# Fifth projection as full-precision products inside attention's first steps, and query norms as multipliers of the scores

## The chip, the cores and the metric

One core of a Trainium2 chip runs the whole program. The time is the device time of one execution in microseconds. TensorE (PE) does matrix products and transposes, VectorE (DVE) and ScalarE (ACT) do elementwise work, GpSimd (POOL) is hardly used, and SyncE (SP) issues the loads.

## The reference, cut to what matters

Two layers, each FFN, hybrid mixer, FFN, over 256 tokens of width 1024. The mixer projects the normed input `u` by `w_in` and splits it:

```python
    (a_q, a_k, a_v, b_cq, b_ckv, b_kr, c_q,
     c_kc, c_vc, c_ks, c_vs, c_kw, c_vw, c_gf) = jnp.split(u @ w_in, splits, axis=-1)
    qa = apply_rope(rms_norm(heads(a_q, A_HEADS), a_qk_g[0]), cos64, sin64)
    ka = apply_rope(rms_norm(heads(a_k, A_KV_HEADS), a_qk_g[1]), cos64, sin64)
...
    qc = rms_norm(heads(c_q, C_HEADS), c_qk_g[0])
    qc_rot = apply_rope(qc, cos64, sin64)
    k_cmp = rms_norm(compress_blocks(...), c_qk_g[1])
    k_slc = apply_rope(rms_norm(heads(c_ks, C_KV_HEADS), c_qk_g[2]), cos64, sin64)
    k_win = apply_rope(rms_norm(heads(c_kw, C_KV_HEADS), c_qk_g[3]), cos64, sin64)
```

Branch a is banded attention with sinks, branch b latent attention, branch c attends to compressed keys (`qc` with `k_cmp`), to selected blocks and to a window (`qc_rot` with `k_slc`, `k_win`). Scores are divided by the root of the head's width before the softmax; a norm of a query is one number per token and head, so it can be applied to the query or to its scores.

## The kernel before, in words

All in fp32. Each engine has one queue, written out by hand, and waits on semaphores; TensorE's products run in the order of its queue. Tokens are two tiles of 128.

The mixer has five projections (`CHUNKS`: F_LAT, F_CMPIN, F_A, F_CQ, F_CK). The first three (`project`, L845) use the fp32 operands as they are; a product of 128x128 by 128x512 is then two instructions. F_CQ (the queries of branch c) and F_CK (its keys and values, 512 columns) use `project_split`: ScalarE rounds the weights into `mwh` quarter by quarter (`round_rows`, L1327), VectorE makes the remainders `mwl` (`rest_rows`, L1915), and TensorE makes three products per block of rounded parts (L861, L862, L866). Both go to PSUM banks 2 and 3. `copy_proj` squares and copies the results for the norms (F_CK: L1277, L1279, into `ck2` and `pk`).

Small products and transposes use banks 4 to 7 as a ring: the names in `AUX` are numbered, number g uses bank 4 + g % 4, and `aux_open` waits until the result of number g - 4 has been taken out by the engine named beside it. The semaphores count in the order of the list. Before the change it has cq0, cq1 (numbers 23, 24), cmps0, cmps1, cr0, cr1, ks, kw, cmpt: transposed cq, compressed scores, transposed roped queries (from `qr`), transposed keys, transposed compressed probabilities.

Attention runs over twelve units n of two heads (two of a, two of b, eight of c). A unit goes through `scores` (TensorE, L890), `rescore` (VectorE, L1980 and L1982: scale, mask and row minimum in one custom operation), `exponents` (ScalarE, L1370 and L1371), `normalise` (VectorE, L1991 to L1997), `turn_probs` (transposes, L901), `turned_probs` (ScalarE's copy, L1378), `values` (L924, L926) and, with its neighbours, `mix_out`, the output projection (L723, L725, L727), whose first piece stands in step n = 4 and waits for `cmpt`. Further work is woven in: in step 1 the compressed scores (L1063) on TensorE and, on VectorE after `rescore(1)`, `key_norms`, then `normalise(1)` and `key_ropes`; in step 2 the transposes of `qr` (L878) and of the keys, and `compressed_scores` (L2020 to L2024) on VectorE after `rescore(2)`; in step 3 `compressed_probs`.

Query and key norms are made by `heads_rstd` (sum of squares, then eight small steps in `rsqrt`) and multiplied in by `by_rstd` (L1510; for cq L1945).

Of the kernel before, what the change touches and what calls it, by code (L numbers as in the profile page):

```python
# [33 lines left out]
I32 = mybir.dt.int32  # L34
# [40 lines left out]
CHUNKS = (F_LAT, F_CMPIN, F_A, F_CQ, F_CK)  # L75
# [6 lines left out]
       ("cq0", "act"), ("cq1", "act"), ("cmps0", "dve"), ("cmps1", "dve"), ("cr0", "act"), ("cr1", "act"),  # L82
# [28 lines left out]
def hybrid_kernel(nc, x, c, positions, ada_w, ada_b, norm_g, ffn_w_in, ffn_w_out, w_in, w_out,  # L111
                  a_sinks, a_qk_g, b_q_lat_g, b_kv_lat_g, b_w_uq, b_w_ukv, b_qk_nope_g, b_qk_rope_g,
                  c_qk_g, c_cmp_pe, c_cmp_w1, c_cmp_w2, c_gate_w, c_gate_b, consts, out):
    with ExitStack() as ctx:
# [122 lines left out]
        def ET(n, i):  # L237
# [6 lines left out]
        csc = fa[:, :, 0:C_H * NCMP].rearrange("p a (h b) -> p a h b", h=C_H)  # L244
        trg = cqT[:, 0:3, :].rearrange("p a n -> p (a n)")
        kwt = sb("kwt", [P, SEQ])
        cst16 = sb("cst16", [P, 3, NT * C_H])
# [35 lines left out]
        muh_ready, mul_ready_, mwh_ready, mwl_ready, mwh_used = (  # L283
            sem(n) for n in ("muh_ready", "mul_ready_", "mwh_ready", "mwl_ready", "mwh_used"))
# [46 lines left out]
        def quarter_at(l, fill, q):  # L331

            return 8 * l + (0 if fill == F_CQ else 4) + q + 1
# [9 lines left out]
        PREP = ["lat", "qb", "kb", "qa", "kc", "cq", "cr", "ck", "cmp"]  # L343
# [38 lines left out]
        def head(n, i):  # L382
# [3 lines left out]
            if br == "a":  # L386
                return (qaT[half, hh // 2, :], kaT[half, hh // 2, :],
                        lambda t: pa[:, t, 384 + hh // 2 * HD:384 + hh // 2 * HD + HD], cst[:, C_BAND:C_CAUSAL + P], SC64)
            if br == "b":
                return qbT[:, hh, :], kbT[:, hh, :], lambda t: kvb[:, t, hh, HD:P], mlate[:, :], SC96  # L390
# [4 lines left out]
                    lambda t: pk[:, t, off:off + HD], mlate[:, :], SC64)  # L395
# [13 lines left out]
        def _(sp):  # L409
# [21 lines left out]
            def ffn_wide(l, f, b, c):  # L431
# [4 lines left out]
                elif f == 1:  # L436
                    sp.wait_ge(proj, projected(l, (F_CQ, F_CK)[b]))
# [169 lines left out]
        def _(pe):  # L607
# [225 lines left out]
            def project(l, fill, width, banks):  # L833
# [4 lines left out]
                if c >= 2:  # L838

                    pe.wait_ge(pcopy, l * 2 * len(CHUNKS) + 2 * (c if fill == F_CK else c - 1))  # L840
# [10 lines left out]
            def project_split(l, fill, banks):  # L851

                n, c = WIDE_M + fill, CHUNKS.index(fill)
                pe.wait_ge(pcopy, l * 2 * len(CHUNKS) + 2 * (c if fill == F_CK else c - 1))
                pe.wait_ge(muh_ready, l + 1)
                pe.wait_ge(mul_ready_, l + 1)
                for q in range(4):
# [12 lines left out]
                    if q < 3 and fill == F_CQ:  # L870
                        i.then_inc(mwh_used, 1)
# [73 lines left out]
            def mixer(l):  # L945
# [3 lines left out]
                pe.wait_ge(pcopy, l * 10 + 4)  # L949
# [74 lines left out]
                turn(l, "kc", [(P * g, kcd[:, g, :, :].rearrange("p a n -> p (a n)")) for g in range(2)])  # L1024
                pe.wait_ge(*aux_done("ka", l))
                pe.wait_ge(pcopy, l * 10 + 6)
                scores(l, 0)
                project_split(l, F_CK, 2)
                cq = pq[:, :, :].rearrange("p t (a n) -> p t a n", a=C_H)

# [1080 lines left out]
```

## Time and profile before

| | |
|---|---|
| median of 3 runs | 1129.51 us (1128.81 to 1130.82) |
| the profiled execution | 1130.08 us, of which 1128.3 is the span |
| TensorE busy | 1084.1 us (96%) |
| VectorE busy | 831.3 us (74%) |
| ScalarE busy | 499.5 us (44%) |
| granted TensorE clock | 0.989 |

Times in the rows are in us from the start of the span, durations in us unless marked ns. A matmul's record is longer than the distance to the next, since they overlap: the rate is read from starts. "PEclk" is the granted share of TensorE's full clock. Idle time in brackets is the engine's own before the instruction, with what ended it.

### The profile page before, as it was taken

What the parts mean: (1) busy time and instruction counts of PE and PEld (TensorE: products, weight loads), DVE (VectorE), ACT (ScalarE), POOL (GpSimd) and SP (SyncE); (2) the same over time, 40 slices, a digit from 0 to 9 for tenths busy, and PEclk for the clock granted to TensorE, in tenths of its full rate; (3) what the DMA queues carried; (4) which work ended last, traced back from release to release, by engine and by line L of the source; (5) the groups of instructions that cost most, each with busy time, mean ns of one, the idle gap of its engine ahead of it and who ended that gap; (6) DMA issues with size and microseconds to landing.
All of it is one profiled execution on the core that took longest, in us unless ns stands there. A gap on an engine that the chain in (4) does not pass through costs nothing.

```text
span 1128.3 us, 13797 instructions
## 1 busy us (share of the span) xinstructions
PE 1084.1 (96%) x5221; PEld 837.4 (74%) x5221; DVE 831.3 (74%) x1502; ACT 499.5 (44%) x868; POOL 12.0 (1%) x30
## 2 busy tenths in 40 slices
PE   5999999999989999999999999999998999999998
PEld 1688888865766588888878888886576667888887
DVE  1766997886988785876687789886879787655644
ACT  2543342324567563343534433422255566433431
POOL 4000000000000000000000000000000000000000
PEclk9999999999989999999999999999998999999999
DMA  9799999454612179896439999954582113876631
GB/s 360 259 378 363 372 378 326 148 180 129 224 62 76 38 252 330 305 325 209 162 113 334 342 387 384 355 194 156 115 294 80 53 61 115 269 250 230 199 112 74
DMA packets 149366, 253.70 MB, mean 225 GB/s; under 512 B 9639, under 2 KB 119861, under 8 KB 141109
## 3 DMA queue, kind: packets, MB, share of 16 engines
q1 hardware_dynamic: 148596, 251.53, 65.1%
q10 hardware_dynamic: 704, 1.30, 0.3%
q8 instruction: 41, 0.67, 0.2%
q14 instruction: 25, 0.20, 0.1%
HBM read 251.76 MB, written 1.05 MB: 224 GB/s over the span
## 4 chain that ended last, share of the span: by engine, by line
PE 84%; DVE 11%; ACT 2%; issue 1%; DMA 1%; SPq 0%; DVEq 0%; ACTq 0%
PE ps L693 12%; PE ps L695 12%; PE ps L694 12%; PE ps L723 8%; PE ps L727 8%; PE ps L725 8%; PE ps L845 6%; DVE mwl L1915 2%; PE ps L705 2%; PE ps L674 1%; PE ps L672 1%; PE ps L673 1%; PE ps L901 1%; DMA wide<-in_ada_w_dram 1%; PE ps L890 1%
## 5 line engine op out<-in xcount | busy, mean ns | idle before, releaser
L693 PE MATMUL ps<-wh,uh 128*128 128x512 f32 x576 | 227.2, 395 | 0.0
L695 PE MATMUL ps<-wlo,uh 128*128 128x512 f32 x576 | 224.5, 390 | 0.0
L694 PE MATMUL ps<-wh,ul 128*128 128x512 f32 x576 | 224.3, 389 | 0.0
L1645 DVE TENSOR_TENSOR wlo<-wide,wh 128x1024 fp32r<-128x1024 f32 x176 | 207.6, 1220 | 15.7 <-ACT wh L1183 13.9
L1183 ACT CAST wh<-wide 128x1024 fp32r<-128x1024 f32 x176 | 175.9, 1049 | 16.7 <-DMA wide<-in_ffn_w_in_dram 16.7
L1255 ACT ACTIVATE fs<-ps 128x512 f32<-128x512 f32 x40 | 24.0, 599 | 282.3 <-PE ps L695 273.1
L1800 DVE TENSOR_TENSOR fa<-fs,ps 128x512 f32<-128x512 f32 x40 | 27.5, 688 | 137.8 <-ACT fs L1255 137.2
L723 PE MATMUL ps<-th,fh 128*128 128x512 f32 x320 | 128.1, 400 | 0.0
L695 PEld LDWEIGHTS ps<-wlo,uh 128*128 128x128 f32 x576 | 108.1, 188 | 23.0
L727 PE MATMUL ps<-tlo,fh 128*128 128x512 f32 x320 | 125.0, 390 | 0.0
L725 PE MATMUL ps<-th,fl 128*128 128x512 f32 x320 | 124.6, 390 | 0.0
L694 PEld LDWEIGHTS ps<-wh,ul 128*128 128x128 f32 x576 | 108.3, 188 | 21.6
L693 PEld LDWEIGHTS ps<-wh,uh 128*128 128x128 f32 x576 | 108.2, 188 | 21.4
L1673 DVE TENSOR_TENSOR tlo<-tall,th 128x1024 fp32r<-128x1024 f32 x104 | 123.4, 1219 | 0.0
L1656 DVE SCALAR_TENSOR_TENSOR acc<-ada,cond,acc 128x2048 f32<-128x2048 f32 (+1 forms) x49 | 100.2, 2044 | 22.9 <-DMA ada<-in_ada_w_dram 22.5
L1190 ACT CAST th<-tall 128x1024 fp32r<-128x1024 f32 x104 | 105.2, 1051 | 10.8 <-DMA tall<-in_ffn_w_out_dram 10.8
L725 PEld LDWEIGHTS ps<-th,fl 128*128 128x128 f32 x320 | 60.2, 188 | 12.7 <-issue 1.0
L727 PEld LDWEIGHTS ps<-tlo,fh 128*128 128x128 f32 x320 | 60.0, 188 | 12.8
L723 PEld LDWEIGHTS ps<-th,fh 128*128 128x128 f32 x320 | 60.1, 188 | 12.6 <-issue 1.0
L845 PE MATMUL ps<-wide,u 128*128 128x416 f32 (+2 forms) x192 | 68.6, 515 | 0.3
L845 PEld LDWEIGHTS ps<-wide,u 128*128 128x128 f32 x192 | 36.0, 190 | 29.5 <-issue 23.6
L1195 ACT CAST fh<-ps 128x512 fp32r<-128x512 f32 x40 | 23.5, 587 | 60.3 <-PE ps L705 60.3
(363 smaller groups left out, 1548.2 us busy)
## 6 DMA issues: line engine op xcount, KB each, us to landing
wide<-in_ffn_w_in_dram SPq DMA_DIRECT2D x176, 512.0 KB, 6.6
ada<-in_ada_w_dram SPq DMA_DIRECT2D x60, 1024.0 KB, 7.1
tall<-in_ffn_w_out_dram SPq DMA_DIRECT2D x44, 1024.0 KB, 5.2
wide<-in_w_in_dram SPq DMA_DIRECT2D x14, 1024.0 KB, 7.5
tall<-in_w_out_dram SPq DMA_DIRECT2D x8, 1024.0 KB, 8.6
ada<-in_ada_w_dram SPq DMA_DIRECT2D x16, 512.0 KB, 5.9
wide<-in_c_cmp_w_dram SPq DMA_DIRECT2D x4, 1024.0 KB, 10.1
wide<-in_w_in_dram SPq DMA_DIRECT2D x4, 832.0 KB, 7.9
```

Source lines behind the costliest of these rows:

```text
L693: mm(o, uh[:, k, rows_], wh[:, hsl, :, k, :], start=(k == 0), stop=False, skip_group_check=True)
L694: mm(o, ul[:, k, rows_], wh[:, hsl, :, k, :], start=False, stop=False, skip_group_check=True)
L695: i = mm(o, uh[:, k, rows_], wlo[:, s, :, k, :], start=False, stop=(k == KD - 1), skip_group_check=True)
L723: mm(y[:, t, hf, :], hi[:, toks], th[:, slot, a, cols], start=(first and x == 0), stop=False, skip_group_check=True)
L725: mm(y[:, t, hf, :], lo[:, toks], th[:, slot, a, cols], start=False, stop=False, skip_group_check=True)
L727: i = mm(y[:, t, hf, :], hi[:, toks], tlo[:, slot, a, cols], start=False, stop=(last and x == len(rows) - 1), skip_group_check=True)
L845: i = mm(ps[:, banks + t, 0:width], u[:, k, t * P:(t + 1) * P], wv[:, k, :], start=(k == 0), stop=(k == KD - 1))
L1183: nc.scalar.copy(wh[:, (n + 1) % 2, :, 2 * c:2 * c + 2, :], raw).then_inc(wh_ready, 1)
L1190: nc.scalar.copy(th[:, n % 2, m % 2, :], tall[:, n % 2, m % 2 * DM:(m % 2 + 1) * DM]).then_inc(th_ready, 1)
L1645: tt(wlo[:, n % 2, :, ks, :], raw, wh[:, (n + 1) % 2, :, ks, :].bitcast(F32), ALU.subtract)\
L1656: stt(part, piece, cond[:, k:k + 1], part, ALU.mult, ALU.add).then_inc(ada_used, 1)
L1673: tt(tlo[:, n % 2, m % 2, :], tall[:, n % 2, m % 2 * DM:(m % 2 + 1) * DM], th[:, n % 2, m % 2, :].bitcast(F32), ALU.subtract).then_inc(tl_ ...
```

## The change

F_CK leaves `CHUNKS`. Its roundings, remainders and split products are gone, and `key_rows` makes it of plain fp32 products in the ring's banks, one tile per name: ck0 after `scores(0)`, ck1 in step 1 after the compressed scores. `copy_keys` takes them out on ScalarE. `AUX` becomes cq0, cq1, ck0, cmps0, cmps1, ck1, cr0, cr1, ks, kw, cmpt (numbers 23 to 33). The cq transposes move ahead of `scores(0)`.

The queries of a and c stay unnormed. `score_root` makes minus the reciprocal root of the sum of squares (the scale of the scores included) into `aroot` and `qroot`, and `rescore` takes it as a per-token multiplier. For the compressed scores it is multiplied in as a tensor, and maximum becomes minimum. Keys of a are still normed, with a table factor of -8.

```diff
-CHUNKS = (F_LAT, F_CMPIN, F_A, F_CQ, F_CK)
+CHUNKS = (F_LAT, F_CMPIN, F_A, F_CQ)
...
-       ("cq0", "act"), ("cq1", "act"), ("cmps0", "dve"), ("cmps1", "dve"), ("cr0", "act"), ("cr1", "act"),
+       ("cq0", "act"), ("cq1", "act"), ("ck0", "act"), ("cmps0", "dve"), ("cmps1", "dve"), ("ck1", "act"), ("cr0", "act"), ("cr1", "act"),
...
-        csc = fa[:, :, 0:C_H * NCMP].rearrange("p a (h b) -> p a h b", h=C_H)
+        csc = ada[:, 0, 0:NT * C_H * NCMP].rearrange("p (a h b) -> p a h b", a=NT, h=C_H)
...
-                    sp.wait_ge(proj, projected(l, (F_CQ, F_CK)[b]))
+                    sp.wait_ge(*((proj, projected(l, F_CQ)), (aux_ready, aux_at(l, "ck1")))[b])
...
+            def key_rows(l, t):
+
+                name = f"ck{t}"
+                bank = aux_open(l, name)
+                n = WIDE_M + F_CK
+                wv = wide[:, n % 2, :].rearrange("p (k n) -> p k n", k=KD)
+                if t == 0:
+                    wide_wait(pe, l, n)
+                for k in range(KD):
+                    i = mm(bank, u[:, k, token(t)], wv[:, k, :], start=(k == 0), stop=(k == KD - 1))
+                i.then_inc(aux_ready, 1)
...
+                pe.wait_ge(pcopy, l * 8 + 8)
+                cq = pq[:, :, :].rearrange("p t (a n) -> p t a n", a=C_H)
+                pairs("cq0", cq, (0, 1))
+                pairs("cq1", cq, (2, 3))
                 pe.wait_ge(*aux_done("ka", l))
                 scores(l, 0)
-                project_split(l, F_CK, 2)
+                key_rows(l, 0)
                 for n in range(1, NU + 3):
...
-                    if n == 1:
-                        pe.wait_ge(prep, prep_at(l, "cq"))
-                        pairs("cq0", cq, (0, 1))
-                        pairs("cq1", cq, (2, 3))
-                        pe.wait_ge(pcopy, l * 10 + 10)
...
+                        key_rows(l, 1)
                     if n == 2:
                         pe.wait_ge(prep, prep_at(l, "ck"))
...
+            def copy_keys(l, t):
+
+                aux_wait(l, f"ck{t}")
+                src = ps[:, aux_bank(f"ck{t}"), :].rearrange("p (a b n) -> p a b n", a=2, b=2)
+                A(ck2[:, t, :].rearrange("p (a n) -> p a n", a=2), src[:, :, 0, :], ACT.Square)
+                nc.scalar.copy(pk[:, t, :].rearrange("p (b a n) -> p a b n", a=2, b=2), src).then_inc(aux_act, 1)
...
-                for q in range(3):
-                    round_rows(F_CK, q)
...
-                round_rows(F_CK, 3)
-
+                out_of(l, "cq0", cqT[:, 0:2, :])
+                out_of(l, "cq1", cqT[:, 2:4, :])
...
-                copy_proj(l, 4)
+                copy_keys(l, 0)
...
+                        if n == 1 and i == 1:
+                            copy_keys(l, 1)
...
+            def score_root(root, sums):
+
+                p, a, n, d = sums.shape
+                link(V.tensor_reduce(ssb[:, 0:a * n].rearrange("p (a n) -> p a n", a=a), sums, AX.X, ALU.add))
+                link(ts(ssb[:, 0:a * n], ssb[:, 0:a * n], HD * EPS, None, ALU.add))
+                rsqrt(a * n, root=root[:, :])
+                return root[:, :].rearrange("p (a n) -> p a n", a=a)
...
-                tt(c[:, 0, :, :], cs64[:, 0, :, :], g(0, HD), ALU.mult)
+                stt(c[:, 0, :, :], cs64[:, 0, :, :], by, g(0, HD), ALU.mult, ALU.mult)
...
-                heads_rstd(qk, HD, v4(qk2[:, :, :], 6))
-                by_rstd(qk, qk)
+                root = score_root(aroot, v4(qk2[:, :, :], 6))[:, :, A_H:6].unsqueeze(3).broadcast_to([P, NT, A_KV, HD])
+                link(tt(qk[:, :, A_H:6, :], qk[:, :, A_H:6, :], root, ALU.mult))
...
-                for q in range(3):
-                    rest_rows(F_CK, q)
                 copied(l, 3)
                 cq = v4(pq, C_H)
-                heads_rstd(cq, HD, v4(cq2[:, :, :], C_H))
...
-                tt(cq, cq, r, ALU.mult).then_inc(prep, 1)
-                dve.wait_ge(prep, prep_at(l, "cq"))
-                rest_rows(F_CK, 3)
+                roots = score_root(qroot, v4(cq2[:, :, :], C_H))
...
-                    V.tensor_tensor_reduce(e[:, 0:P], ps[:, i, 0:P], cst[:, C_CAUSAL:C_CAUSAL + P], -scale, least,
+                    V.tensor_tensor_reduce(e[:, 0:P], ps[:, i, 0:P], cst[:, C_CAUSAL:C_CAUSAL + P], scale[0], least,
...
                 def key_norms():
-                    copied(l, 4)
+                    dve.wait_ge(*aux_done("ck1", l))
...
-                    link(V.tensor_reduce(over(0), csc, AX.X, ALU.max))
+                    link(tt(csc, csc, roots.unsqueeze(3).broadcast_to([P, NT, C_H, NCMP]), ALU.mult))
+                    link(V.tensor_reduce(over(0), csc, AX.X, ALU.min))
```

## Rows read from the trace of the kernel before

**Rows 1.** The page, busy time, share of the span, instructions.

```profile
PE 1084.1 (96%) x5221; PEld 837.4 (74%) x5221; DVE 831.3 (74%) x1502; ACT 499.5 (44%) x868; POOL 12.0 (1%) x30
```

**Rows 2.** The chain of waits by time, 225 to 335: start, us, what.

```profile
260.00 13.93 PE ps L845 x32
...
292.93 3.50 DVE mwl L1915 x3
296.43 1.14 DVE ssb L1503
...
299.48 1.24 DVE acc L1945
300.74 1.23 DVE mwl L1915
...
305.81 0.35 DVE acc L1980
...
308.88 0.17 DVE stat L1991
...
331.68 0.48 ACT cmpT L1295
```

**Rows 3.** Timeline of TensorE: start, us, engine, line, count, [idle before].

```profile
295.41 0.93 PE L890 MATMUL ps<-kaT,qaT 64*128 64x128 f32 x8 [1.57 <-ACT kaT L1295]
...
311.40 2.65 PE L1063 MATMUL ps<-kcT,cqT 64*128 64x15 f32 x32 [0.47 <-ACT cqT L1295]
...
314.68 2.77 PE L890 MATMUL ps<-kbT,qbT 96*128 96x128 f32 x8
317.24 1.91 PE L878 MATMUL ps<-cst,qr 128*128 128x128 f32 x8
...
319.97 0.55 PE L901 MATMUL ps<-cst,early 128*128 128x128 f32 x3
...
332.25 0.47 PE L723 MATMUL ps<-th,uh 128*128 128x512 f32 x1 [2.20 <-ACT cmpT L1295]
```

**Rows 4.** Windows: length, then busy time of each engine, granted clock, DMA share.

```profile
312.00:320.00 8.00, 8.00 (x53) 6.84 (x51) 7.47 (x32) 3.45 (x12) 0.00 (x0) 0.57 0.43 138
320.00:332.00 12.00, 7.87 (x61) 5.49 (x59) 11.46 (x50) 9.56 (x30) 0.00 (x0) 1.00 0.01 1
332.00:337.00 5.00, 4.75 (x15) 3.71 (x15) 2.72 (x10) 1.41 (x6) 0.00 (x0) 0.66 0.00 0
337.00:382.00 45.00, 43.64 (x277) 29.77 (x276) 35.93 (x134) 30.14 (x83) 0.00 (x0) 1.00 0.21 71
```

**Rows 5.** Timeline of VectorE.

```profile
249.34 0.88 DVE L1858 TENSOR_SCALAR latT<-ps,latg 128x256 f32<-128x256 f32 x2 [0.16 <-PE ps L878]
...
281.49 2.36 DVE L1915 TENSOR_TENSOR mwl<-wide,mwh 128x1024 fp32r<-128x1024 f32 x2 [2.72 <-ACT mwh L1327]
...
311.09 0.68 DVE L1503 TENSOR_REDUCE ssb<-ck 128x8 f32<-128x512 f32 x1
...
320.11 0.47 DVE L2020 TENSOR_TENSOR fa<-ps,cst 128x120 f32<-128x120 f32 x2
...
322.16 0.15 DVE L1992 RECIPROCAL stat<-stat 128x2 f32<-128x2 f32 x1
```

**Rows 6.** Timeline of ScalarE.

```profile
293.78 0.60 ACT L1287 COPY acc<-ps 128x512 f32<-128x512 f32 x1
...
309.75 0.57 ACT L1279 COPY acc<-ps 128x512 f32<-128x512 f32 x1
...
320.56 0.48 ACT L1378 COPY acc<-ps 128x384 f32<-128x384 f32 x1 [0.78 <-PE ps L901]
...
321.82 0.39 ACT L1370 ACTIVATE acc<-acc,stat 128x128 f32<-128x128 f32 x1
```

**Rows 7.** Groups by form, 286 to 332: count, busy, mean ns of one.

```profile
L1980 DVE CUSTOM_DVE_ANT_0 acc<-ps,cst,nsink 128x128 f32<-128x128 f32 x2 | 0.7, 350 | 0.0
...
L1980 DVE CUSTOM_DVE_ANT_0 acc<-ps,cst 128x128 f32<-128x128 f32 x2 | 0.6, 290 | 0.0
```

More of the change, by code:

```diff
@@ L282, in hybrid_kernel @@
         chain_s = sem("chain")
-        muh_ready, mul_ready_, mwh_ready, mwl_ready, mwh_used = (
-            sem(n) for n in ("muh_ready", "mul_ready_", "mwh_ready", "mwl_ready", "mwh_used"))
+        muh_ready, mul_ready_, mwh_ready, mwl_ready = (
+            sem(n) for n in ("muh_ready", "mul_ready_", "mwh_ready", "mwl_ready"))
         gu_t0, ft_t0, fh_t0, fl_t0 = (sem(n) for n in ("gu_t0", "ft_t0", "fh_t0", "fl_t0"))
@@ L331, in quarter_at @@
         def quarter_at(l, fill, q):
-            return 8 * l + (0 if fill == F_CQ else 4) + q + 1
+            return 4 * l + q + 1
         def row_at(l, j, t):
@@ L387, in head @@
                 return (qaT[half, hh // 2, :], kaT[half, hh // 2, :],
-                        lambda t: pa[:, t, 384 + hh // 2 * HD:384 + hh // 2 * HD + HD], cst[:, C_BAND:C_CAUSAL + P], SC64)
+                        lambda t: pa[:, t, 384 + hh // 2 * HD:384 + hh // 2 * HD + HD], cst[:, C_BAND:C_CAUSAL + P],
+                        [aroot[:, 6 * t + hh:6 * t + hh + 1] for t in range(NT)])
             if br == "b":
-                return qbT[:, hh, :], kbT[:, hh, :], lambda t: kvb[:, t, hh, HD:P], mlate[:, :], SC96
+                return qbT[:, hh, :], kbT[:, hh, :], lambda t: kvb[:, t, hh, HD:P], mlate[:, :], [-SC96, -SC96]
             win = int(br == "win")
@@ L394, in head @@
             return (crT[half, hh // 2, :], ckT[half, 2 * win + kv, :],
-                    lambda t: pk[:, t, off:off + HD], mlate[:, :], SC64)
+                    lambda t: pk[:, t, off:off + HD], mlate[:, :],
+                    [qroot[:, C_H * t + hh:C_H * t + hh + 1] for t in range(NT)])
         def head_at(l, n, i):
@@ L1324, in round_rows @@
                     act.wait_ge(wide_in[n % 2][q // 2], wide_at(l, n))
-                    if fill == F_CK and q < 3:
-                        act.wait_ge(mwh_used, 3 * l + q + 1)
                     nc.scalar.copy(mwh[:, ks, :], wide[:, n % 2, :].rearrange("p (k n) -> p k n", k=KD)[:, ks, :])\
@@ L1400, in mixer @@
                             act.wait_ge(cmp_shift, l + 1)
-                            A(csc, csc, ACT.Exp, scale=SC64).then_inc(cmp_exp, 1)
+                            A(csc, csc, ACT.Exp, scale=-1.0).then_inc(cmp_exp, 1)
                         if n == 4 and i == 0:
@@ L1483, in link, with rsqrt @@
                 dve.wait_ge(chain_s, chain["n"])
-            def rsqrt(n, p=P):
-                s, t, r = ssb[0:p, 0:n], newt[0:p, 0:n], rst[0:p, 0:n]
-                link(ts(r.bitcast(I32), s.bitcast(I32), -0.5, float(0x5F3759DF), ALU.mult, ALU.add))
+            def rsqrt(n, p=P, root=None):
+                s, t, r = ssb[0:p, 0:n], newt[0:p, 0:n], rst[0:p, 0:n] if root is None else root
+                seed = float(0x5F3759DF) if root is None else float(0x5F3759DF - 2 ** 31)
+                link(ts(r.bitcast(I32), s.bitcast(I32), -0.5, seed, ALU.mult, ALU.add))
                 link(tt(t, r, r, ALU.mult))
@@ L1979, in rescore @@
                         dve.wait_ge(pt_ready, head_at(l, n - 2, i))
-                    V.tensor_tensor_reduce(e[:, 0:P], ps[:, i, 0:P], cst[:, C_CAUSAL:C_CAUSAL + P], -scale, least,
+                    V.tensor_tensor_reduce(e[:, 0:P], ps[:, i, 0:P], cst[:, C_CAUSAL:C_CAUSAL + P], scale[0], least,
                                            ALU.add, ALU.min, st[:, 2:3])
-                    V.tensor_tensor_reduce(e[:, P:3 * P], ps[:, i, P:3 * P], head(n, i)[3], -scale, least,
+                    V.tensor_tensor_reduce(e[:, P:3 * P], ps[:, i, P:3 * P], head(n, i)[3], scale[1], least,
                                            ALU.add, ALU.min, st[:, 3:4]).then_inc(nm_ready, 1)
```

31 lines of the change are left out of this document (10 added, 21 removed).

## The prediction

> **What bounds the kernel now.** I read the page first. TensorE is busy 96% of the span, VectorE 74% [rows 1], so only the stretches in which TensorE stands idle can give time back, and an added TensorE wait costs time wherever it stands. Next the chain of waits, in order of time, in the first layer's mixer; the second layer repeats it 546 us later. It runs through TensorE up to the projection of 260.00 (16 products, 32 instructions, 13.93 us), then mostly through VectorE from 281 until the copy of cmpT at 331.68 [rows 2], which releases the first matmul of the output projection at 332.25 after 2.20 us of idle [rows 3]. From 337 to 382 TensorE is busy 43.64 of 45 us [rows 4]: whatever delays 332.25 delays the end by as much.
>
> The timelines of the engines between 292 and 332 then tell what each step costs. Of VectorE's time there, the change removes the fifth projection's remainders (three from 292.93, 3.50 us, and one at 300.74, 1.23) and the multiplication of cq by its norm (299.48, 1.24) [rows 2]. These are on the chain, so the change looks like a gain. Whether it is one depends on what VectorE waits for next: the key rows, which it begins to norm at 311.09 [rows 5].
>
> **Part 1, the key rows.** In full precision the fifth projection is 16 products of 512 columns, and the third projection is that very shape: 13.93 us, so 6.97 per tile [rows 2]. It is not the price alone that counts but the order on TensorE. Worked out for the first layer:
>
> Scores of unit 0 still wait for kaT, so they start at 295.4 as before [rows 3]. The eight cq transposes, moved ahead of them, need the copy of the fourth projection, at 293.78 + 0.60 = 294.4 [rows 6]; they take 1.0 and fit the 1.57 us gap [rows 3]. Cost nothing, with 0.1 at most if qaT's copy holds back the second four. Tile 0 runs from 296.3 to 303.2, scores(1), as long as those of 295.41, to 304.1.
>
> TensorE then wants the normalised probabilities of unit 0. VectorE starts on cq at 294.45 in place of 296.43; the sums and the root take 299.48 - 296.43 = 3.05, the rope and the rest up to the first rescoring 305.81 - (300.74 + 1.23) = 3.84, and from there to the end of the first normalisation 308.88 - 305.81 = 3.07 [rows 2]. With 0.12 for two pointer scalars (part 3) that is 304.5, so TensorE waits 0.4. Transposes of one head 0.4, to 304.9. The compressed scores took 2.6, but the clock was falling in them [rows 3, 4]; I take 2.1, and 1.6 and 2.6 as bounds, half a microsecond to either side. To 307.0. Only now comes tile 1, 6.97, to 314.0. ScalarE squares and copies it in 0.84 (0.57 for the copy [rows 6], 0.27 for the squares, an estimate for half as many elements): ck1 is done at 314.9.
>
> VectorE's key norms wait for exactly that. They started at 311.09 [rows 5] and now start at 314.95: **+3.85 us**. VectorE has finished rescoring unit 1 near 307 and stands some 8 us before the wait; the 6 us that were taken from it lie in that hole. Queued behind the wait are both normalisations of unit 1, the key ropes, the rescoring of unit 2 and the compressed softmax: all of the chain to cmpT. Even both tiles back to back could not have been copied before 296.3 + 13.9 + 0.8 = 311.0, no sooner than now.
>
> **Part 2, the new place in the ring of banks.** Helper banks are reused four names on. The second block of cr now stands four behind cmps0, so its transposes wait until VectorE has added the mask to cmps0. That add stands behind rescore(2), in VectorE's queue at 320.11 [rows 5], now 323.97, done at 324.25. TensorE finishes scores(2) and the first half of cr near 315.8 and stands still for 8.5 us; behind it wait values(0), the transposes of unit 1, ks, kw and scores(3). From 324.25 on at full clock: half of cr 0.45 (a quarter of 1.91, the clock being low there), values 0.8 (from 319.15 to 319.97), one head's transposes 0.45 (0.55 less its overlap) [rows 3], then ScalarE's copy and exponents of (2,0), 321.82 - 320.56 = 1.26 [rows 6]: 327.25 plus 0.1 for the handoffs. VectorE, undisturbed, would ask for it at 322.16 + 3.85 + 0.44 (part 3) = 326.45 [rows 5]. That is +0.9, and 0.25 more, an estimate, as ScalarE needs longer for the second head's exponents than VectorE for normalising the first: **+1.15** at full clock.
>
> The clock decides the rest. After the thin stretch before 312 it was granted at 0.57 on average over 312 to 320, after the thin stretch before 332 at 0.66 over 332 to 337, the lower of the levels being 1.2 GHz of 2.4 [rows 4]; eight transposes took 1.91 us there [rows 3], so four 0.95. Here an idle spell of 8.5 us stands ahead. If the clock is low when TensorE comes back, the three steps take 0.95 + 1.6 + 0.65 in place of 1.7, that is 1.5 more: +2.65. I take this; the first bound is 0, as no row shows a fall behind a single spell of that length, the other 1.3 more should scores(3) be at 1.2 GHz as well (unit 2's were recorded at 2.77 there [rows 3], half of which the full clock would save).
>
> The Trainium skill, page "TensorE: Matmul & The Clock Gate", section "HAM oscillation — how this bites in real kernels", says that a TensorE which pauses long between groups of matmuls begins the next group at the lower clock. It speaks against the change; by it the sum is the one that I take, without it the 1140.6 below. Page "FP8 and Floating Point Precision" of the Trainium skill gives true FP32 four passes, which by a pass of 0.2275 us would make the fifth projection 14.6; the row says 13.93 and stands, the other would add 1.3 to the total.
>
> **Part 3, the norm as a multiplier.** The scores of branches a and c now take a pointer for the scale. A rescoring with one pointer more costs 350 against 290 ns [rows 7]: 0.06 each; a gain is excluded, since the operation is the same but for the pointer. On the chain are the two of unit 4's first head, 0.12; later ones lie under a TensorE that is busy 97% [rows 4]; bare of that cover, 32 of them are 1.9 a layer. The extra multiplication of csc (240 elements) costs what its subtraction costs, 0.41 and a handoff: 0.44, on the chain. Norming 256 elements of qk in place of 768 saves some 0.6 by the size of cq's 1.24, ahead of a wait of 2.72 for the rounded weights [rows 5]: nothing. The tables get a factor in an instruction of the same size: nothing; VectorE has 0.16 us of slack behind them [rows 5], and should each of the 15 cost a pointer's 0.06 more, the bound is 0.8 a layer.
>
> **Part 4, ScalarE and the queues.** Four roundings less for ScalarE: it waited for TensorE between them, nothing. SP's load of the second FFN block waits for ck1 (314.0) in place of the old projection, about 7 us earlier, with the output projection's later rows and the first FFN rows queued behind it; those wait for TensorE's work of 337 and later in any case, and the block itself is used after 390. Nothing; without that cover 7.
>
> **Sum** per layer: 3.85 + 2.65 + 0.44 + 0.12 = 7.06, two layers 14.1. On the profiled execution's 1130.08 us (span 1128.3 and 1.78 around it) this is 1144.2; the median of the runs shown is 0.57 lower, so 1143.6.
>
> **Rivals.** (a) The clock is full when TensorE returns: 5.56 a layer, 1140.6. For it: it held 1.00 from 320 to 332 with 4 us of idle in between [rows 4]. Chance 0.20. (b) It stays low through scores(3): 8.4 a layer, 1146.3; 0.12. (c) The shift of the idle spells spares the output projection's first matmuls the low clock of 332 to 337, where 5 us at 0.66 hold the work of 3.3: 1.7 back a layer, 1140.2; 0.10. (d) The wait behind cmps0 hides altogether: 4.4 a layer, 1138.3; against it stands that VectorE needs values(0) next. 0.05. (e) The other side: VectorE's relief arrives. Removing 3.50 + 1.23 + 1.24 and adding 0.44 gives 5.53 a layer, 1118.4. It decides once tile 1 is copied by 307, when VectorE is free; the order on TensorE puts it at 314.9, and even a gain of nothing needs it at about 310.5. 0.03. (f) No change within 0.2% (2.3 us), about what a measurement can tell: delay and relief would have to cancel; 0.02. My forecast 0.45, the rest 0.03 unnamed and slower. So faster 0.03, same 0.02, slower 0.95. The range goes from (d) at 1138.3, with the lower bound of the compressed scores inside it, to (b) with the 0.5 a layer of their upper bound, 1147.3.
>
> **What would show it.** In the profile of the changed kernel: 32 instructions of the key rows at 0.435 us spacing; a VectorE wait of about 8 us before the key norms, released by ScalarE's pk copy; a TensorE wait of about 8 us at the transposes of qr; the granted clock near 0.5 behind it; the output projection starting near 339.4. Wrong would be: tile 1 done before 310, a short wait at qr, or later idle of TensorE shrinking by what came in here.

## The result, and the profile of the changed kernel

The changed kernel took 1147.11 us (median of 4, 1146.66 to 1150.76) against 1129.71 for the kernel before beside it (1128.81 to 1130.82): ratio 1.016, 95% interval 1.0147 to 1.0173. It is slower by 17.4 us, where 14.1 were forecast: 3.5 above the forecast time. The range ended at 1147.3, and the result lies on that end: the median is 0.2 below it, the mean of the four executions, 1147.9, is 0.6 above it. Its profiled execution took 1150.76 us with a span of 1148.9.

The page of the changed kernel, its line of busy times (compare [rows 1]):

```profile
PE 1093.2 (95%) x5189; PEld 830.6 (72%) x5189; DVE 825.3 (72%) x1494; ACT 491.3 (43%) x860; POOL 12.0 (1%) x30
```

VectorE is busy 6.0 us less and ScalarE 8.2 less: the rounding work is gone. TensorE is busy 9.1 us more with 32 instructions fewer. The span grew by 20.6, so TensorE also stands idle 11.5 us longer. The timeline of TensorE in the first mixer shows where (start, us, engine, line, count, [idle before <- releaser]; compare [rows 3]):

```profile
296.08 1.15 PE L891 MATMUL ps<-cst,acc 128*128 128x128 f32 x8 [0.59 <-ACT acc L1292]
297.16 0.93 PE L903 MATMUL ps<-kaT,qaT 64*128 64x128 f32 x8
...
306.33 0.55 PE L914 MATMUL ps<-cst,acc 128*128 128x128 f32 x3 [0.32 <-DVE acc L2007]
306.81 1.97 PE L1073 MATMUL ps<-kcT,cqT 64*128 64x15 f32 x32
308.70 8.77 PE L883 MATMUL ps<-wide,u 128*128 128x512 f32 x16
...
318.95 0.60 PE L891 MATMUL ps<-cst,qr 128*128 128x128 f32 x4
327.76 1.12 PE L891 MATMUL ps<-cst,qr 128*128 128x128 f32 x4 [8.20 <-DVE ada L2030]
...
332.94 1.48 PE L903 MATMUL ps<-kbT,qbT 96*128 96x128 f32 x8
...
343.04 0.77 PE L726 MATMUL ps<-th,uh 128*128 128x512 f32 x1 [2.32 <-ACT cmpT L1307]
```

The cq transposes lie ahead of the first scores, the second tile at 308.70, and between the two halves of the qr transposes TensorE stands still for 8.20 us until VectorE's L2030 frees the bank. The tile took 8.77 us, not the 6.97 of the forecast. The windows say why (length, busy times, granted clock, DMA share; compare [rows 4]):

```profile
308.00:309.00 1.00, 1.00 (x15) 0.97 (x14) 0.92 (x6) 0.84 (x4) 0.00 (x0) 0.81 0.00 0
309.00:312.00 3.00, 3.00 (x4) 1.21 (x4) 0.00 (x0) 1.40 (x7) 0.00 (x0) 0.50 0.00 0
312.00:314.00 2.00, 2.00 (x6) 0.88 (x5) 0.00 (x0) 0.00 (x0) 0.00 (x0) 0.99 0.00 0
...
323.00:327.00 4.00, 0.00 (x0) 0.00 (x0) 3.93 (x15) 0.00 (x0) 0.00 (x0) 0.50 0.53 175
327.00:333.00 6.00, 5.24 (x27) 4.20 (x28) 3.31 (x13) 2.37 (x9) 0.00 (x0) 0.54 0.00 0
333.00:338.00 5.00, 3.34 (x25) 2.29 (x26) 4.57 (x23) 5.00 (x16) 0.00 (x0) 1.00 0.00 0
```

The clock was at the lower level, 1.2 GHz, from about 308.6 to 312, in the first products of the tile. It fell a second time inside the idle spell, and was still low when TensorE came back. The timelines of VectorE and ScalarE hold the two waits (compare [rows 5, 6]):

```profile
318.41 0.69 DVE L1511 TENSOR_REDUCE ssb<-ck 128x8 f32<-128x512 f32 x1 [9.48 <-ACT acc L1302]
...
327.43 0.47 DVE L2030 TENSOR_TENSOR ada<-ps,cst 128x120 f32<-128x120 f32 x2
327.93 0.41 DVE L2033 TENSOR_TENSOR ada<-ada,qroot 128x240 f32<-128x240 f32 x1
...
332.61 0.17 DVE L2002 RECIPROCAL stat<-stat 128x2 f32<-128x2 f32 x1 [1.33 <-ACT acc L1379]
```

```profile
317.51 0.38 ACT L1301 ACTIVATE ck<-ps 128x256 f32<-128x256 f32 x1 [7.12 <-PE ps L883]
317.80 0.58 ACT L1302 COPY acc<-ps 128x512 f32<-128x512 f32 x1
```

VectorE, ready at 308.9, waits 9.48 us for the second tile's copy: the time that the removed remainders and the removed multiplication gave it is spent there.

To compare executions whose mixers begin at other times, each landmark is taken as its start minus the start of the mixer's first projection product (226.47 in the first layer before, 228.10 after). 1.6 us of the profiled execution's excess lie ahead of the first mixer, where nothing was changed; two later profiles of the same kernel have 226.05 and 226.19 there. The landmarks are the start of the key norms, the normalisation of unit 2's first head, called (2,0) (322.16 before, 332.61 after), the output projection's first matmul, and the two-column matmul that ends it. First layer / second layer:

| kernel | key norms | normalisation (2,0) | output projection starts | it ends |
|---|---|---|---|---|
| before | 84.6 / 84.6 | 95.7 / 95.7 | 105.8 / 105.8 | 156.0 / 156.0 |
| after | 90.3 / 90.4 | 104.5 / 104.6 | 114.9 / 115.0 | 165.1 / 165.3 |
| after, 2nd profile | 88.7 / 88.6 | 102.9 / 102.9 | 113.3 / 113.3 | 162.0 / 163.6 |
| after, 3rd profile | 88.7 / 88.7 | 102.9 / 102.9 | 113.3 / 113.3 | 163.6 / 164.8 |
| norms' part alone | 83.7 / 84.0 | 95.3 / 95.5 | 105.5 / 106.9 | 155.5 / 155.6 |
| bank outside the ring | 90.3 / 88.7 | 101.9 / 100.2 | 113.3 / 111.2 | 162.0 / 161.5 |
| tile first | 86.5 / 86.6 | 100.8 / 100.8 | 111.2 / 111.6 | 159.9 / 161.9 |
| fillers | 90.3 / 88.7 | 103.1 / 101.4 | 113.5 / 111.8 | 162.2 / 160.8 |
| tile first, ring too | 86.6 / 86.5 | 98.1 / 98.1 | 108.7 / 109.5 | 159.1 / 159.5 |
| VectorE's order | 88.6 / 88.6 | 98.4 / 98.4 | 110.1 / 109.5 | 161.6 / 159.8 |
| both of these | 89.2 / 89.2 | 99.0 / 99.0 | 110.1 / 109.6 | 160.4 / 159.9 |
| both tiles together | 86.4 / 86.4 | 97.9 / 97.9 | 108.3 / 108.6 | 158.5 / 158.8 |
| keys' part alone | 94.4 / 91.1 | 108.6 / 105.3 | 119.1 / 115.6 | 169.2 / 165.8 |

At the end of the output projection the excess is 9.2 and 9.3 us in the two layers of the first profile of after. The rows below the third profile are the experiments of the next section, each from one profiled execution.

### The profile page after: what moved, and what is told of

It is laid out like the page before. It is cut to its first block, busy times and chain, and to the rows that moved or that the text cites. A ratio compares the mean times of both kernels' runs of the same rounds, so it can differ in the third digit from the quotient of the medians.

```text
span 1148.9 us, 13705 instructions
## 1 busy us (share of the span) xinstructions
PE 1093.2 (95%) x5189; PEld 830.6 (72%) x5189; DVE 825.3 (72%) x1494; ACT 491.3 (43%) x860; POOL 12.0 (1%) x30
## 3 DMA queue, kind: packets, MB, share of 16 engines
HBM read 251.76 MB, written 1.05 MB: 220 GB/s over the span
## 4 chain that ended last, share of the span: by engine, by line
PE 79%; DVE 12%; DMA 4%; ACT 3%; issue 2%; SPq 0%; DVEq 0%; ACTq 0%
PE ps L696 10%; PE ps L698 10%; PE ps L697 10%; PE ps L726 6%; PE ps L730 6%; PE ps L728 6%; PE ps L848 6%; DMA ada<-in_ada_w_dram 3%; DVE acc L1672 2%; PE ps L883 2%; PE ps L708 1%; PE ps L677 1%; PE ps L675 1%; PE ps L676 1%; PE ps L914 1%
## 5 line engine op out<-in xcount | busy, mean ns | idle before, releaser
L1661 DVE TENSOR_TENSOR wlo<-wide,wh 128x1024 fp32r<-128x1024 f32 x176 | 207.5, 1220 | 16.1 <-ACT wh L1194 14.1
L697 PEld LDWEIGHTS ps<-wh,ul 128*128 128x128 f32 x576 | 108.3, 188 | 21.7
L1672 DVE SCALAR_TENSOR_TENSOR acc<-ada,cond,acc 128x2048 f32<-128x2048 f32 (+1 forms) x49 | 100.2, 2044 | 24.2 <-DMA ada<-in_ada_w_dram 23.9
```

The costliest lines, as they stand in the source:

```text
L697: mm(o, ul[:, k, rows_], wh[:, hsl, :, k, :], start=False, stop=False, skip_group_check=True)
L1661: tt(wlo[:, n % 2, :, ks, :], raw, wh[:, (n + 1) % 2, :, ks, :].bitcast(F32), ALU.subtract)\
L1672: stt(part, piece, cond[:, k:k + 1], part, ALU.mult, ALU.add).then_inc(ada_used, 1)
```

## The experiments

**Is the ring wait real: the second tile's bank outside the ring.** Bank 3 is free then; the cr blocks wait for cq1 and ck0, both long done.

```diff
+        RING = [n for n in AUXN if n != "ck1"]
         def aux_bank(name):
-            return 4 + AUXN.index(name) % 4
+            return 3 if name == "ck1" else 4 + RING.index(name) % 4
```

> The changed kernel, but tile 1 of the key rows is written to bank 3, outside the ring, so the second block of cr stands four behind ck0 and no longer behind cmps0 (ks is the first to wait for cmps0). Theory: the ring wait makes TensorE stand 8.2 us before values(0), and the copy and exponents of unit 2's first head come 2.7 us a layer too late (of it 1.5 by the lower clock, 1.1 by the order). Without it 1147.1 - 5 = 1142, and between 1141 and 1144 if ks, kw and scores(3) then run at the lower clock. Rival, VectorE's own queue sets the pace and the ring wait is hidden in it: within 1 us of 1147.1.

Measured 1141.0 us (1139.86 to 1141.9), ratio 1.0094, interval 1.0077 to 1.0111. Its TensorE timeline in the first layer:

```profile
306.40 8.83 PE L888 MATMUL ps<-wide,u 128*128 128x512 f32 x16
...
316.70 1.04 PE L896 MATMUL ps<-cst,qr 128*128 128x128 f32 x8
...
325.60 1.94 PE L896 MATMUL ps<-cst,krd 128*128 128x128 f32 x8 [4.63 <-DVE ada L2035]
...
327.97 2.73 PE L908 MATMUL ps<-kbT,qbT 96*128 96x128 f32 x8
```

All eight qr transposes run at once. From the key norms to the normalisation (2,0) it is 11.5 us, against 14.2 in the changed kernel and 11.1 before: up to that landmark the ring wait cost 2.7 us a layer, as expected. The tile is slow here in the first layer (8.83 us, key norms at 90.3) and not in the second (88.7), which is one reason why the time is 1 us below the expected 1142. Part of the gain is given back. TensorE now waits 4.63 us ahead of the transposes of the keys, the clock granted over 323 to 328 is 0.57, and the scores of unit 3 take 2.73 us here and 2.32 in the second layer, where they took 1.48 in the changed kernel. From the normalisation to the output projection it is 11.4 and 11.0 us in place of 10.4, so counted up to there the ring wait cost 1.7 and 2.1 us a layer.

**The second tile ahead of the compressed scores,** with the ring's order of banks kept as in the changed kernel, so that the ring wait stays.

```diff
                     if n == 1:
+                        key_rows(l, 1)
                         pe.wait_ge(*aux_done("kc", l))
...
-                        key_rows(l, 1)
```

> The changed kernel, but tile 1 of the key rows stands before the compressed scores on TensorE; banks and their waits as in the changed kernel. Theory A, the clock falls because of the small products and transposes of step 1 (compressed scores above all) and slows tile 1 from 6.97 to 8.6 us: tile 1 is done 1.9 + 1.65 = 3.5 us sooner in each layer, 1147.1 - 7 = 1140. Theory B, the fp32 products themselves let the clock fall: the fall comes inside tile 1 again, only the 1.9 of the order is won, 1143.3.

Measured 1141.67 us (1140.11 to 1141.86), ratio 1.0096, interval 1.0076 to 1.0116. TensorE, first layer:

```profile
306.38 7.03 PE L886 MATMUL ps<-wide,u 128*128 128x512 f32 x16
313.34 1.96 PE L1077 MATMUL ps<-kcT,cqT 64*128 64x15 f32 x32
...
323.69 1.12 PE L894 MATMUL ps<-cst,qr 128*128 128x128 f32 x4 [6.16 <-DVE ada L2033]
```

The tile took 7.03 us in both layers. Key norms are 1.9 us late instead of 5.7, and the ring wait is still there, 6.16 us; the normalisation comes 14.2 us behind the key norms, as in the changed kernel. Against the first profile of the changed kernel the key norms, the normalisation and the output projection's start all come 3.8 us sooner in the first layer: a delay of the tile passes one for one to what stands behind it. The time lies between what the two theories gave, 1140 and 1143.3. The tile at the higher clock speaks for theory A, but does not show it, since two later profiles of the changed kernel have the tile at 7.13 us in its old place too. Against those, the order alone saves 2.1 us a layer.

**The clock behind the idle spell: 34 filler matmuls in it,** between the two cr blocks, so that TensorE comes back at the higher level.

```diff
                         pairs("cr0", qr, (0, 1))
+                        keep_warm(34, 3)
                         pairs("cr1", qr, (2, 3))
```

> The changed kernel with 34 bf16 products of 512 columns (7.3 us) into the idle bank 3 where TensorE stands still before the second block of cr. They compute nothing. Theory: the clock stays full through cr, values(0) and the transposes of unit 1, 1.5 us a layer: 1147.1 - 3 = 1144; a little less if the last of them end behind the wait. Rival, what makes the steps behind the wait long is the handoffs and not the clock: 1147 or more.

Measured 1141.46 us (1138.95 to 1142.13), ratio 1.0094, interval 1.0075 to 1.0114. TensorE and the windows:

```profile
318.97 7.29 PE L616 MATMUL ps<-zb 128*128 128x512 bf16 x33
327.12 0.66 PE L891 MATMUL ps<-cst,qr 128*128 128x128 f32 x4 [0.87 <-DVE ada L2031]
...
340.91 0.47 PE L726 MATMUL ps<-th,uh 128*128 128x512 f32 x1 [2.32 <-ACT cmpT L1308]
```

```profile
307.00:313.00 6.00, 6.00 (x28) 3.19 (x27) 1.24 (x6) 2.23 (x10) 0.00 (x0) 0.72 0.01 3
322.00:331.00 9.00, 8.13 (x53) 5.11 (x52) 7.66 (x30) 2.49 (x9) 0.00 (x0) 1.00 0.31 96
339.00:345.00 6.00, 4.09 (x23) 3.08 (x23) 4.47 (x17) 3.44 (x12) 0.00 (x0) 1.00 0.00 0
```

The second half of the qr transposes starts at the same landmark as in the changed kernel (99.7 us, and there too the tile was slow), the normalisation comes 3.4 us behind it instead of 4.85: the lower clock cost 1.5 us there. The gain on the result's median, 5.6 us, is more than these 3.0 of two layers. In the profile the tile was spared the lower clock in the second layer (key norms at 88.7), and the output projection took 48.7 and 49.0 us in the two layers, against 50.2 and 50.3 in the first profile of the changed kernel; in the first layer the clock was at 1.00 over 339 to 345, where before the change 332 to 337 had 0.66 [rows 4]. That the fillers brought these two about is not shown: the second profile of the changed kernel has both in its first layer without a filler.

**The norms' part alone,** on the kernel before: roots as multipliers in the score pass and on csc, factors in the tables, the fifth projection as it was.

```diff
-                heads_rstd(cq, HD, v4(cq2[:, :, :], C_H))
-                tt(cq, cq, r, ALU.mult).then_inc(prep, 1)
+                roots = score_root(qroot, v4(cq2[:, :, :], C_H))
...
-                    V.tensor_tensor_reduce(e[:, 0:P], ps[:, i, 0:P], cst[:, C_CAUSAL:C_CAUSAL + P], -scale, least,
+                    V.tensor_tensor_reduce(e[:, 0:P], ps[:, i, 0:P], cst[:, C_CAUSAL:C_CAUSAL + P], scale[0], least,
```

> The kernel before with the second half of the change alone: norms as multiplier of the scores, the fifth projection still split in three rounded products. Theory: VectorE's chain loses the multiplication of cq (1.24), of which TensorE's projection (done at 307.3) and the rescoring of unit 1 let about 1.1 through, and gains 0.44 for csc and 0.12 for pointers: -0.5 a layer, 1128.7 against 1129.7. Rival, the pointers of all later units (1.9 us a layer) come through: 1132 or more. If this is right, the whole loss of 17.4 us belongs to the key rows and their places.

Measured 1130.62 us (1126.05 to 1134.62, 10 runs), ratio 1.0, interval 0.9984 to 1.0016: no difference that these runs can tell, and the expected gain of 1 us in all lies inside the interval. The profiled execution has some 0.4 us a layer of it: the output projection ends at 155.5 and 155.6 instead of 156.0. The rival, 1132 or more, did not come true.

**VectorE's order.** The compressed scores are masked, multiplied and reduced ahead of the key norms, in VectorE's hole.

```diff
                     if n == 1:
+                        compressed_scores()
                         ck = key_norms()
-                    if n == 2:
-                        compressed_scores()
```

> The changed kernel with one thing moved: in step 1 VectorE masks, multiplies and reduces the compressed scores ahead of the key norms, in the hole in which it waits for the second tile's copies, and no longer in step 2. Theory (two terms: key norms late behind the second tile, ring wait behind the compressed scores' bank): the bank is free before the key norms start, so the ring wait goes as it went in the run with the second tile's bank outside the ring, and about 1.9 us of VectorE work leaves the path as well: key norms still start 5.7 us late, the normalisation of unit 2's first head some 10.5 us behind them, 1139.5 us in all. Rival (the ring wait only stood in for another wait, by ScalarE's copies or the exponents, that is due as early): as the changed kernel, 1145 or more. Second rival (VectorE's work there lay beside waits anyway): as with the bank outside the ring, 1141.

Measured 1139.67 us (1139.59 to 1141.54), ratio 1.0087, interval 1.0071 to 1.0103. VectorE, first layer:

```profile
307.39 0.47 DVE L2030 TENSOR_TENSOR ada<-ps,cst 128x120 f32<-128x120 f32 x2
...
315.31 0.69 DVE L1511 TENSOR_REDUCE ssb<-ck 128x8 f32<-128x512 f32 x1 [6.13 <-ACT acc L1302]
```

The add that held the bank runs at 307.39, ahead of the wait, and the ring wait is gone. The normalisation comes 9.8 us behind the key norms. The time is the one expected, the way to it is not: the key norms were only 4.0 us late, since the tile took 7.13 us in both layers, and the normalisation was due at 98.4, not at some 101. Of that gain 1.6 and 1.0 us are given back in the two layers before the output projection starts (11.7 and 11.1 us between the two in place of 10.1), as with the bank outside the ring: the scores of unit 3 take 2.77 and 2.18 us.

**Both terms at once: tile first in the ring too.** As "tile first", with ck1 ahead of cmps0 in AUX as well, so that the cr blocks wait for what is long done.

```diff
-("ck0", "act"), ("cmps0", "dve"), ("cmps1", "dve"), ("ck1", "act"), ("cr0", "act"), ("cr1", "act"),
+("ck0", "act"), ("ck1", "act"), ("cmps0", "dve"), ("cmps1", "dve"), ("cr0", "act"), ("cr1", "act"),
```

> The changed kernel with the second tile of the key rows ahead of the compressed scores, in its products and in the ring's order as well (tile, compressed scores, then the turned rows), so that both terms shrink at once. Theory (the terms add): key norms 1.9 us later than before the change as in the run with the tile first, the unit 2 normalisation 11.5 us behind them as in the run with the bank outside the ring, 98.1 us behind the mixer's first projection product where it was 95.7 before; 2.4 to 2.7 us per layer, 1135 us. Rival (the two terms are one wait seen twice): no better than either alone, 1141.

Measured 1137.64 us (1134.09 to 1138.06), ratio 1.0057, interval 1.0039 to 1.0074. The landmarks are those expected, 86.5 and 98.1: the two terms add. The time is 2.6 us above the one expected; 1.9 of them lie between the normalisation and the output projection, which takes 10.7 and 11.4 us here in the two layers against 10.1 before. The scores of unit 3 lie there, with 2.23 and 2.77 us in place of 1.48.

**Both orders together,** tile first in the ring too and VectorE's compressed scores ahead of the key norms.

> The run with the second tile first in products and ring, and VectorE's compressed scores ahead of the key norms as well. They end on TensorE about 1 us behind the tile, so VectorE waits about as long for them as for the key copies: key norms start 1.0 to 2.0 us later than with the tile first alone, and step 2 is 1.9 us shorter. Theory: within 1 us of that run either way, 1134 to 1136. Rival (step 2's VectorE work was the bound there): 1132.

The expectation was 1134 to 1136. Measured 1138.24 us (1136.57 to 1140.64), ratio 1.0075, interval 1.0051 to 1.0098: the key norms start 2.7 us later than with the tile first in the ring too, more than the 1 to 2 expected, and step 2 gets back 1.7. Nothing is gained.

**No tile inside step 1: both tiles between the scores of units 0 and 1.**

```diff
                 key_rows(l, 0)
+                key_rows(l, 1)
...
-                        key_rows(l, 1)
```

> The changed kernel with both tiles of the key rows one behind the other between the scores of units 0 and 1, where the kernel before had its whole fifth projection. No tile lies inside step 1, and nothing waits for one there. Theory: the products take 14.0 us where the three-product form took about 12.0, so the scores of unit 1 start at 84.0 us behind the mixer's first projection product (80.9 before), the key norms at 87.2 (84.6 before), all clocks as before: 2.6 to 3.1 us per layer, 1135.5 us. Rival (what costs is the place inside step 1 and not the fp32 products, since ScalarE's and VectorE's rounding is gone): as before the change, 1130.

Measured 1136.36 us (1134.63 to 1137.97), ratio 1.0053, interval 1.0033 to 1.0074. TensorE and VectorE:

```profile
295.48 14.00 PE L883 MATMUL ps<-wide,u 128*128 128x512 f32 x32
309.40 0.93 PE L903 MATMUL ps<-kaT,qaT 64*128 64x128 f32 x8
```

```profile
310.37 0.41 DVE L1989 CUSTOM_DVE_ANT_0 early<-ps,cst,nsink 128x128 f32<-128x128 f32 x1 [5.58 <-PE ps L903]
...
311.96 0.68 DVE L1510 TENSOR_REDUCE ssb<-ck 128x8 f32<-128x512 f32 x1
```

VectorE does not wait at the key norms: its wait, 5.58 us, now lies ahead of the rescoring of unit 1, for the scores of that unit. They start 83.8 us behind the mixer's start, 80.9 before the change. Nearly all of that is the price of the form, as the starts on TensorE show, the first product of the fifth projection and the scores of unit 1 behind it, before the change:

```profile
296.27 0.50 PE L861 MATMUL ps<-mwh,muh 128*128 128x512 f32 x1
...
307.38 0.93 PE L890 MATMUL ps<-kaT,qaT 64*128 64x128 f32 x8
```

The 48 instructions of the old form took 11.1 us from the first start to that of the scores (the expectation had some 12.0), the 32 of the new one take 13.9: 2.8 a layer and 5.6 in all, of the 6.4 measured. None of the full-precision orders that were tried beats the kernel before. This one has the lowest median, but it cannot be told from the tile first in the ring too (ratios 1.0053 and 1.0057).

**The keys' part alone.** Both tiles as in the changed kernel; query norms and the cq transposes in their old form, the latter back in step 1.

```diff
-                roots = score_root(qroot, v4(cq2[:, :, :], C_H))
+                heads_rstd(cq, HD, v4(cq2[:, :, :], C_H))
...
+                    if n == 1:
+                        pe.wait_ge(prep, prep_at(l, "cq"))
+                        pairs("cq0", cq, (0, 1))
+                        pairs("cq1", cq, (2, 3))
```

> The keys' part alone, the complement of the run with the norms alone: both full-precision tiles at the changed kernel's places and in its ring; query norms multiplied into the query rows as before the change, the query transposes of the compressed branch back in step 1 (0.9 us ahead of the compressed scores), no multiplication by the square roots. Theory (nearly all of the loss is the keys' part): key norms start 6 to 6.5 us late, the ring wait is there at 2.2 to 2.7, less the 0.4 of the multiplication that is gone: 8.3 to 9 us per layer, 1146.5 us, or 1144 where the clock holds its higher level in the second tile. Rival (the two parts cost together what neither costs alone): 1138 or less.

Measured 1151.87 us (1149.0 to 1154.63), ratio 1.0181, interval 1.0157 to 1.0205, 5 us above what was expected. TensorE, first layer:

```profile
306.66 2.83 PE L1072 MATMUL ps<-kcT,cqT 64*128 64x15 f32 x32 [1.05 <-ACT cqT L1306]
309.42 9.57 PE L881 MATMUL ps<-wide,u 128*128 128x512 f32 x16
```

In the second layer the tile took 7.1 us and the key norms are 6.5 late, at the upper end of what was expected; in the first the lower clock covered the compressed scores too, and they are 9.8 late. So the keys' part holds the whole loss. The norms' part, worth nothing that was measured on the kernel before, gives back some 2.5 us a layer once the tile stands behind the compressed scores (91.1 against 88.7). The timeline puts most of it on the cq transposes (0.9 us) and the wait for their copy (1.05), which then no longer stand ahead of the tile.

**The changed kernel again,** unchanged, measured twice more, on two chips.

> The changed kernel as it is, profiled and timed again on one chip with the run beside it. If the low clock in the second tile belongs to the order of the instructions, the tile takes 8.7 us in both layers again and the time is 1147. If it comes in some executions and not in others (of eight second tiles behind the same instructions, in four profiled kernels, four took 8.7 to 8.8 us and four 7.1), the profile may show 7.1 in one layer or in both, key norms then 4.0 late, and the unprofiled times scatter between 1143.5 and 1148.

> The changed kernel as it is, a third time, to see how its time goes with the clock that each execution was granted. Theory (the second tile, and what lies around it, is at the lower clock in some executions only): an execution with a mean granted clock of 0.985 takes 1146.5 to 1148, one of 0.988 to 0.990 takes 1143 to 1145, and nothing lies far from these two; the median falls on one of them or between. Rival (the 3.5 us between the two measurements are something else, memory say, or the chip): the time doesn't go with the clock.

The second measurement gave 1143.63 us (1143.13 to 1144.49), ratio 1.0113, interval 1.0098 to 1.0128; the third 1147.0 (1146.19 to 1148.55), ratio 1.0157, interval 1.0144 to 1.0171. TensorE in the second's profile, and its window over the tile:

```profile
304.75 1.96 PE L1073 MATMUL ps<-kcT,cqT 64*128 64x15 f32 x32
306.64 7.13 PE L883 MATMUL ps<-wide,u 128*128 128x512 f32 x16
...
324.05 1.12 PE L891 MATMUL ps<-cst,qr 128*128 128x128 f32 x4 [8.19 <-DVE ada L2030]
...
339.33 0.47 PE L726 MATMUL ps<-th,uh 128*128 128x512 f32 x1 [2.32 <-ACT cmpT L1307]
```

```profile
309.00:310.00 1.00, 1.00 (x4) 0.47 (x3) 0.00 (x0) 0.00 (x0) 0.00 (x0) 1.00 0.00 0
...
339.00:341.00 2.00, 1.67 (x7) 1.42 (x8) 1.93 (x6) 1.50 (x6) 0.00 (x0) 1.00 0.04 8
```

The windows of the third, over both layers' first output projection matmuls:

```profile
339.00:343.00 4.00, 3.53 (x9) 2.85 (x10) 3.06 (x10) 1.63 (x6) 0.00 (x0) 0.57 0.02 4
...
893.00:898.00 5.00, 4.88 (x12) 3.85 (x13) 2.70 (x9) 1.28 (x6) 0.00 (x0) 0.50 0.00 0
898.00:903.00 5.00, 5.00 (x32) 3.51 (x31) 2.81 (x11) 3.47 (x10) 0.00 (x0) 0.87 0.00 0
```

Of the 13 executions of the changed kernel in the three measurements, the nine at a mean granted clock of 0.985 or 0.986 took 1146.19 to 1150.76, the four at 0.988 to 0.990 took 1143.13 to 1144.49. So the time goes with the clock. The four at the higher clock are all of one measurement on one chip, and these thirteen alone don't part the clock from the chip. Two other kernels, each on one chip, do: the keys' part alone took 1152.9 and 1154.6 us at 0.985 and 0.984 but 1150.8 and 1149.0 at 0.988, and both tiles together 1137.9 and 1138.0 at 0.989 but 1134.6 and 1134.8 at 0.994. The 4.6 us between the lowest and the highest of the nine don't go with the mean clock. Nor is the place always the tile: in the third profile it ran at the higher level in both layers (7.13 us), and the lower level lay on the output projection, from start to end 50.3 and 51.6 us against 48.7 where it was spared (second profile, first layer) and 50.2 before the change.

## Why the prediction was right in direction and too small in size

**The step that failed is in part 1: "Only now comes tile 1, 6.97".** The tile was priced at the full clock, with no bound and no rival for the lower one, although [rows 4] had the clock at 0.57 over 312 to 320, within and behind the compressed scores. In the profile of the result it met the lower level in both layers: 8.77 us in the first, in place of the 7.13 of the profiles where it was spared. The key norms were 5.69 us late, not 3.85; in the two profiles where the tile was spared, 4.0. That is 1.65 a layer and 3.3 in all, in the first profile. The prediction gave the lower clock four places (the compressed scores, behind the spell, scores(3), the output projection), never the first products of the tile. The mechanism, VectorE waiting for a tile that comes late in TensorE's order, was right; the size of the term was not. Everything else up to the tile held. The scores of unit 0 moved by 0.1, TensorE waited 0.32 us for the probabilities (0.4 forecast), the compressed scores took 1.97 (2.1), ScalarE's copies 0.87 (0.84).

For the median the same holds with one reserve. The executions of the result at 0.985 had as much of the lower clock as its profiled one (0.985), but only the profiled one shows where, and the third profile, with the tile spared, lost 2.9 us against the second in the two output projections. What is shown is that 3.5 us separate medians of identical instructions and go with the granted clock; that all of it lay on the tile in the unprofiled executions is not. In the third profile, 1146.19 us, the forecast missed by another term, part 4's "nothing" for the output projection: it took 51.6 us in the second layer, 1.4 more than before the change, since the lower clock lasted longer in it. That the second measurement, 1143.63, falls on the forecast of 1143.6 is partly luck: its path to the output projection was 7.5 us a layer longer in the profile, where 7.06 were forecast, and 1.5 us were saved in the first layer's output projection, which the sum did not count.

**Part 2 was right in mechanism and size, up to the normalisation.** L2030 released the transposes after 8.20 us (8.5 forecast). From the key norms to the normalisation the path grew by 3.13 us, against 2.65 + 0.44. The bank outside the ring measures the wait at 2.7, the fillers the clock in it at 1.5, as taken. Up to the output projection the wait is worth less, 1.7 and 2.1, since without it the scores of unit 3 meet the lower clock. That the clock would be low at the return, rival (a) against, held in all three profiles of the changed kernel.

**Part 3 was right in kind, and its 0.12 too small.** The multiplication of csc took 0.41. The first rescorings show the pointer, in the groups by form (count, busy, mean ns; compare [rows 7]):

```profile
L1990 DVE CUSTOM_DVE_ANT_0 acc<-ps,cst,nsink 128x128 f32<-128x128 f32 x2 | 0.8, 408 | 0.0
...
L1990 DVE CUSTOM_DVE_ANT_0 acc<-ps,cst 128x128 f32<-128x128 f32 x2 | 0.6, 288 | 0.0
```

408 ns in place of 350 with one pointer more, 288 where there is none. From the normalisation to the output projection the path grew by 0.33 to 0.36, where 0.12 was forecast. The reliefs and the tables' factors moved nothing ahead of the first scores (69.06 against 68.94).

**Part 4** holds: from the output projection's start to its end it is 50.2 us in the first layer of before and of after, so neither SP's earlier load nor the later rescorings show there.

**The rivals.** (c), the output projection spared the lower clock, is what the second profile's first layer did (1.5 us, 1.7 forecast). (b), at 1146.3 the rival nearest to the result, did not happen: in all three profiles of the changed kernel the scores of unit 3 took 1.48 us in both layers, the clock being full again. Where the number came near, it was by the tile. (d) fell with the ring experiment and (e) with VectorE's wait of 9.48 us. The signs named held: 32 instructions, VectorE waiting (9.48, about 8 forecast), TensorE waiting 8.2 at qr, clock 0.50 behind it. The output projection, forecast for 339.4, which is 112.9 behind the mixer's start, came at 114.9, and at 113.3 in the two profiles with the tile at full clock.

**What the loss is made of.** 6.4 of the 17.4 us stay in the order without a tile in step 1, and 5.6 of them are the price of the form itself. The rest is the order: the tile behind the compressed scores, the bank behind their release, and the clock that both meet.

## What to carry to other kernels

Before crediting a removed VectorE job, look up what VectorE waits for next and when TensorE delivers it in its own order; here 6 us of relief became a 9.5 us wait. When a name is put into a ring of buffers, list for each later name whose release it now waits for, and where that release stands in its engine's queue. Where the trace of before shows the lower clock in a stretch that the change reorders, price each group of products there at both levels: the difference here was up to 1.7 us a place, and it was not the same from one execution to the next.

## What was not expected of the hardware

The clock fell in the middle of nearly uninterrupted work, and not always. Behind the same instructions (scores of unit 1, three transposes, 32 compressed score products of 15 columns) the second tile was at the lower level at its start in 4 of 12 passages (six profiled kernels with that order, two layers each): twice in the first profile of after, none in the other two, once each with the bank outside the ring and with the fillers, none with VectorE's order. Between tile 0 and tile 1 TensorE stood idle for 0.32 us in the first profile and for 0.31 in the second. What makes the difference was not found out.

Taking a long wait away moved the lower clock instead of removing it. In the changed kernel, with its 8.2 us wait at the qr transposes, the clock was full again by the scores of unit 3: 1.48 us in all six passages (with the tile first, where that wait is 6.16 us, 1.48 and 1.77). In the five variants of it that run all eight qr transposes at once (bank outside the ring, VectorE's order, tile first in the ring too, both of these, both tiles together) TensorE waits 2.8 to 4.6 us ahead of the transposes of the keys, and the scores of unit 3 took 1.70 to 2.77 us in all ten passages. With the fillers they took 1.48, and the way from the normalisation to the output projection was as long as in the changed kernel, 10.4 us. No run tested this alone.
